# A mixture-of-experts loop on one core: all transposes of a block moved together, ahead of its two column-grouped products

## What is computed

```python
def swiglu(x, wg, wu, wd):
    return (jax.nn.silu(x @ wg) * (x @ wu)) @ wd
...
def expert_block(args):
    tok, e = args
    return swiglu(h_pad[tok], w_e_gate[e], w_e_up[e], w_e_down[e])
...
out = jnp.zeros((M + 1, D), ys.dtype).at[row_tok].add(ys * row_w[:, None])
```

## Time and profile before

| | |
|---|---|
| time, median of 3 runs | 2286.18 us (2284.29 to 2286.26) |
| the profiled execution: time / span | 2279.32 us / 2277.5 us |
| TensorE busy | 2106.7 us (93%) |
| VectorE busy | 1377.6 us (60%) |
| ScalarE busy | 1044.5 us (46%) |
| GpSimd busy | 1027.4 us (45%) |
| mean granted TensorE clock | 0.966 of full |
| experts' loop | from about 1362 us to the end |

### The profile page before, as it was taken

How to read it: one execution, slowest core, us unless ns; L and a number is a source line. 1 busy time by engine, 2 the same in 40 slices (tenths; PEclk the granted TensorE clock), 3 DMA queues, 4 the chain that set the end, 5 groups by cost and what they waited for, 6 DMA issues and landing times. The chain is left out here.

```text
span 2277.5 us, 42891 instructions
## 1 busy us (share of the span) xinstructions
PE 2106.7 (93%) x15302; PEld 1585.9 (70%) x15302; DVE 1377.6 (60%) x2383; ACT 1044.5 (46%) x1582; POOL 1027.4 (45%) x851
## 2 busy tenths in 40 slices
PE   7999799969799989999898789999999999999994
PEld 6777667747444458888687537777777777777773
DVE  3488778875576662111367426777767777777772
ACT  6321222166666661111233105666666666666662
POOL 2111222242577741110016515677666666776662
PEclk9999999979899999999999899999999999999997
DMA  6587711064655557882433068999999999999996
GB/s 220 168 270 250 252 47 38 22 198 135 205 168 167 160 165 259 284 286 66 172 122 103 10 227 292 339 344 328 329 333 345 332 337 339 335 338 335 342 325 156
DMA packets 178690, 520.62 MB, mean 229 GB/s; under 512 B 22907, under 2 KB 77354, under 8 KB 152142
## 3 DMA queue, kind: packets, MB, share of 16 engines
q1 hardware_dynamic: 130646, 359.62, 44.9%
q0 software_dynamic: 37520, 97.81, 16.9%
q10 hardware_dynamic: 10416, 61.82, 8.1%
HBM read 442.31 MB, written 125.08 MB: 249 GB/s over the span
## 5 line engine op out<-in xcount | busy, mean ns | idle before, releaser
L2689 DVE TENSOR_TENSOR w_gu_lo<-turned,w_gu_hi 128x2048 fp32r<-128x2048 f32 x132 | 302.7, 2294 | 133.3 <-ACT w_gu_hi L2611 133.3
L2611 ACT ACTIVATE w_gu_hi<-turned 128x2048 fp32r<-128x2048 f32 x132 | 254.0, 1925 | 41.1 <-PEq L1896 41.1
L612 PE MATMUL pP<-wring,hT_hi 128*128 128x512 f32 (+2 forms) x576 | 227.6, 395 | 20.7 <-DVE wring L547 11.3
L614 PE MATMUL pP<-wring,hT_lo 128*128 128x512 f32 (+2 forms) x576 | 222.2, 386 | 0.0
L613 PE MATMUL pP<-wring,hT_hi 128*128 128x512 f32 (+2 forms) x576 | 222.1, 386 | 0.0
L2538 PE MATMUL pG_e<-w_gu_hi,xT_hi 128*128 128x512 f32 x528 | 214.6, 407 | 0.0
L2538 PE MATMUL pG_e<-w_gu_lo,xT_hi 128*128 128x512 f32 x528 | 208.9, 396 | 0.0
L2538 PE MATMUL pG_e<-w_gu_hi,xT_lo 128*128 128x512 f32 x528 | 208.7, 395 | 0.0
L2465 POOL DMA_INDIRECT x_scratch<-turned,target x66 | 106.9, 1620 | 203.0 <-ACT turned L2652 199.2
L476 ACT ACTIVATE stage<-pP 128x512 f32<-128x512 f32 (+3 forms) x72 | 41.1, 571 | 305.6 <-PE pP L614 299.0
L388 POOL TENSOR_TENSOR wring<-turned,wring 128x512 fp32r<-128x512 f32 (+1 forms) x43 | 70.6, 1673 | 225.4 <-ACT wring L422 225.4
(11 more groups left out here) (332 smaller groups left out, 5075.4 us busy)
## 6 DMA issues: line engine op xcount, KB each, us to landing
turned<-in_w_e_gate SPq DMA_DIRECT2D x66, 1024.0 KB
turned<-in_w_e_up SPq DMA_DIRECT2D x66, 1024.0 KB
turned<-in_w_e_down SPq DMA_DIRECT2D x66, 1024.0 KB
turned<-in_cache_sb_kv SPq DMA_DIRECT2D x256, 256.0 KB, 3.1
out<-in_cache_win_kv ACTq DMA_DIRECT2D x8, 4094.0 KB
turned<-in_w_in ACTq DMA_DIRECT2D x56, 256.0 KB, 6.0
turned<-in_w_in SPq DMA_DIRECT2D x16, 512.0 KB, 7.5
out<-in_cache_win_kv ACTq DMA_DIRECT2D x8, 1022.0 KB
```

What stands on the lines that cost most here:

```text
L612: pe.matmul(pP[:m, i % 4, :w], hi, w_hi(u), start=(c == 0), stop=False)
L614: last = pe.matmul(pP[:m, i % 4, :w], lo, w_hi(u), start=False, stop=(c == KC - 1))
L2611: act.activation(ghi[:, r, k, :, :].rearrange("p c f -> p (c f)"), w[:, r, k, :], ACT.Copy).then_inc(ghi_ready, 1)
L2689: dve.tensor_tensor(glo[:, r, k, :, :].rearrange("p c f -> p (c f)"), w[:, r, k, :], ghi[:, r, k, :, :].rearrange("p c f -> p (c f)").bitc ...
```

## The change

On TensorE, `turn_hidden` of the block before, `turn_tail` and `turn_rows` of the next block now stand together behind `down`, and the two tail products stand together behind them: `turn_hidden(j-1)`, `turn_tail(j+1)`, `turn_rows(j+1)`, `down_tail(j-2)`, `gate_up_tail(j)`, `gate_up(j)`, `down(j-1)`. ACT and DVE split the turned rows ahead of the tail's gate instead of behind it. Nothing is added or removed, and the loads, gathers and scatters stay where they stand in their own queues.

```diff
@@ TensorE
                 def body(it, which):
                     for j in range(U):
-                        turn_next = which != "last" or j < U - 1
-                        if turn_next:
+                        if which != "first" or j > 0:
+                            turn_hidden(it, j - 1)
+                        if which != "last" or j < U - 1:
                             turn_tail(it, j + 1)
+                            turn_rows(it, j + 1)
+                        if which != "first" or j > 1:
+                            down_tail(it, j - 2)
                         gate_up_tail(it, j)
-                        if turn_next:
-                            turn_rows(it, j + 1)
                         gate_up(it, j)
                         if which != "first" or j > 0:
                             down(it, j - 1)
-                        turn_hidden(it, j)
-                        if which != "first" or j > 0:
-                            down_tail(it, j - 1)
@@ TensorE, behind the loop
                 body(last, "last")
+                turn_hidden(last, U - 1)
+                down_tail(last, U - 2)
                 down(last, U - 1)
                 down_tail(last, U - 1)
@@ ScalarE
                     for j in range(U):
-                        gate_tail(it, j)
                         if which != "last" or j < U - 1:
                             rows_high(it, j + 1, 0)
                             rows_high(it, j + 1, 1)
+                        gate_tail(it, j)
+                        if which != "last" or j < U - 1:
                             gu_high(it, j + 1, 0)
@@ VectorE
                     for j in range(U):
+                        if which != "last" or j < U - 1:
+                            rows_low(it, j + 1, 0)
+                            rows_low(it, j + 1, 1)
                         gate_tail(it, j)
                         if which != "last" or j < U - 1:
                             take_tail(it, j + 1)
-                            rows_low(it, j + 1, 0)
-                            rows_low(it, j + 1, 1)
                             gu_low(it, j + 1, 0)
```

## The result

The changed kernel takes 2293.16 us (median of 12 runs, 2287.81 to 2297.09) against 2286.06 us for the one before, run beside it (12 runs): ratio 1.0034, 95% interval 1.0024 to 1.0045. It is slower by 7 to 8 us. The forecast was a gain of 7.5 us; what came is close to the slower rival, C. The profiled execution has a span of 2289.7 us against 2277.5. That is more than the change did: from the first `turn_hidden` to the last it is 2253.72 - 1386.42 = 867.3 us against 2241.90 - 1381.84 = 860.1, 7.2 us more, and most of the rest stands ahead of the loop.

A forecast was written before the change was run, and what follows sets the result against it. TensorE was taken to bound the loop, the DMA engines close behind. A gain of 9.5 us (0.15 us in 63 blocks) less 2 us lost at `put` made 7.5: 2286.18 - 7.5 = 2278.7 us, range 2274.5 to 2287.

The forecast's parts named there:

- Rival C: Down weights asked for 1.07 us later make scatter, `put` and `turn_hidden` late: 6 us slower, 2292 us; chance 0.14.
- What bounds the kernel: In the experts' loop TensorE sets the pace, 13.25 us a block, with the DMA engines close behind.
- Rival B: The DMA engines hold the loop's pace, only 0.03 to 0.08 us a block spare: 2283 us; chance 0.22.
- TensorE's sum: TensorE from `turn_hidden` to `gate_up`: 4.61 us against 4.76, 0.15 less a block, 63 times, 9.5 us.
- Rival D: The 0.15 us at L2576 comes from ending four side-by-side products and stays: nothing gained, 2286 us; chance 0.14.
- The late requests: Down load 1.07 us later, gate and up 0.7; scatters some 0.5 later would give back 2 us at `put`.
- The limit: Latest harmless start of `put` after `turn_hidden`: 6.17 us before the change, 6.02 with TensorE 0.15 quicker.
- GpSimd's held `target` copy: VectorE's two-input instructions keep GpSimd from reading SBUF; a `put` slipping past one such hold may slip by the next.
- ScalarE's and VectorE's order: The small tail gate moves behind the two splits of the rows, both behind `put`; costed at nothing.
- the earlier turns: `turn_tail` wants its gathered rows a microsecond sooner, 0.58 after `turn_hidden` instead of 1.58; TensorE never waited for them.
- The ends of the loop: First and last blocks: at worst one `gate_up_tail` of 2 us loses its cover, once; costed at nothing.

The follow-up runs named there:

- e3: The changed kernel with two buffers for the results `y` and `y_tail` instead of one; 0.9964 of the kernel before.
- e9: The kernel before with two result buffers instead of one; 0.9998 of the kernel before.
- e4: Against the kernel before, TensorE's two tail products together but `turn_rows` left behind them, ScalarE and VectorE as before; 0.9975, 2279.74 us.
- e1: The changed kernel with `down_tail` put back right behind `turn_hidden`, ahead of the next block's turns; 1.0030 of the kernel before.
- e13: The changed kernel with half of the up weights, a block's last load, left out (another output); 0.9966 of the kernel before.
- e14: The kernel before with half of the up weights, a block's last load, left out (another output); 0.9990 of the kernel before.
- e7: The kernel before with the change's order on ScalarE and VectorE alone, TensorE as before; 1.0006 of the kernel before.
- e11: The changed kernel with half of the down weights, a block's first load, left out (another output); 0.9975 of the kernel before.
- e12: The kernel before with half of the down weights, a block's first load, left out (another output); 0.9999 of the kernel before.

## Why the prediction was wrong, step by step

**What bounds the kernel: right.** TensorE does, and the DMA engines were close behind, but not as engines that are full: e3 runs at 13.18 us a block with the same share of 1.02. Rival B is out.

**TensorE's sum: right in kind, too large.** The groups measured 0.31, 0.27, 0.27, 0.97, 0.88 and 1.95 us against 0.31, 0.27, 0.24, 0.98, 0.85 and 1.96: L2500 to L2511 costs 0.03 more than the row ahead of the loop had it, and L2576 to L2525 keeps 0.03 of its loss. That makes 4.65 instead of 4.61 and a gain of 0.10 to 0.11 us a block instead of 0.15, some 6.5 us. e3 over e9 gives 0.34%, 7.8 us by their medians, though their blocks differ by 0.07 us, 4.4 us in 63; the intervals of the two allow for either. Rival D is out: L2576 to L2525 is 0.88 and not 1.00. The Trainium skill's rule (TensorEngine Tiling (Array Packing), Key Properties), that a change of mode drains TensorE and a change of tile does not, agrees with the trace: L2576 holds TensorE for 0.88 us ahead of another product in its mode and for 1.00 ahead of a transpose. e4 with as few changes (13.11 at the shortest) and e1 with as many as before (13.29) bear it out in kind; the rule does not explain the 0.05 us by which e1 is above the kernel before.

**The late requests: the step that failed.** I had `down_tail` later by 1.07 us (measured: 1.24 at the down load) and the gate load later by 0.7 (measured: 1.03 to 1.14; it left 0.7 us behind the start of `gate_up`, where I had reckoned with the 0.3 of before; why is open). Then I wrote: "If the later loads make scatters land some 0.5 us later, a fifth of the blocks pass the limit by 0.15 us or so. That is 13 x 0.15 = 2 us given back". The shift of 0.5 us had no row behind it. `put` moved by 1.26 us, the whole of the delay, and the loss is 0.23 us a block, 14 us where I had 2. The limit itself was right: 6.02 was the forecast, and the `put` at 7.28 made its block 1.22 longer than 13.15, so 6.06 was free. 19 of 52 `put`s came later than that, up to 1.22 us, where I had a fifth of them and 0.15 us.

**Rival C had it**, path and price: a mean stall of 0.25 us (0.23 measured) and 2292 us, at a chance of 0.14. But it named the down load, and e1, with that load on time and gate and up late, is as slow as the change (1.0030). That C's time came out so close is in part luck: the stall was a guess, and TensorE's gain under it was 0.10 us, not 0.15. What I set against C, that a scatter need not wait for the whole of the loads, is what e13 and e14 refute. The profile held a warning that I read as comfort: `put` waited for the scatter in 26 of 53 blocks of the kernel before, so half of the blocks had nothing between the landing and `put`, and any delay of the landing had to pass on in full there. GpSimd's held `target` copy (Trainium skill, SBUF — State Buffer, Who interferes with whom) played no part in it: in the changed kernel the copy took 0.20 us on average, where before it was 1.14 (1.39 in the earlier trace rows), and it released `put` in 4 of 52 blocks.

**ScalarE's and VectorE's order, the earlier turns: right.** Nothing that can be measured (e7), and TensorE never waits for gathered rows in the changed kernel between 1500 and 2200 us. **The ends of the loop: nearly.** No run has them alone. From the first L2511 to the first `turn_hidden` it is 19.89 us in the changed kernel against 19.03, where kernels with TensorE's old order have 19.0 to 19.6; so they cost up to 0.9 us, and not nothing.

## What to carry to other kernels

When a product is moved later, follow what its end releases beyond the next engine: here a buffer's release is a load's request, the loads form a row, and the scatter on another queue lands only behind the last of that row. A load that has microseconds to spare before its own reader can still be the one that sets the pace. Look for circles through a single buffer (`put`, scatter, landing, `put`), ask what stretches each of their legs, and hold the whole against the period that you aim at (13.15 us here). Such a circle is best broken by a second buffer before the period is shortened, and the second buffer shows nothing until then (0.9998, e9).

## What the runs showed of the hardware that was not expected

The DMA share is no gauge of room. Leaving out 11% of the bytes (e11: 299 GB/s instead of 334) took it from 1.02 to 1.00:

```profile
1500.00:2200.00 700.00, 698.75 (x7002) 557.29 (x7001) 496.16 (x534) 458.35 (x533) 475.64 (x319) 1.00 1.00 299
```

And where the bytes are left out matters as much as how many. In the kernel before, the same 0.5 MB a block moved `put` by 2.4 us when taken from the last load (e14) and not at all when taken from the first (e12); in the changed kernel it is 1.7 us (e13) and 0.7 us (e11).
